# Gated delta rule: the queries' decay factors come as one row per head through memory, and VectorE multiplies them in at level 0 of the inverse

## What is computed

```python
gc = jnp.cumsum(to_chunks(g, l), axis=-1)          # log decays, summed within a chunk
...
sol = lax.linalg.triangular_solve(a_mat + jnp.eye(l), rhs, left_side=True, lower=True, unit_diagonal=True)
u, w = sol[..., :dv], sol[..., dv:]
qk = jnp.where(incl, jnp.einsum('bhnid,bhnjd->bhnij', qc, kc) * dmat, 0.0)
q_dec = qc * jnp.exp(gc)[..., None]                # the queries with their decay
...
def step(s, inp):
    v_new = u_i - jnp.einsum('bhck,bhkv->bhcv', w_i, s)
    o = jnp.einsum('bhck,bhkv->bhcv', q_i, s) + jnp.einsum('bhij,bhjv->bhiv', qk_i, v_new)
```

## Time and profile before

| | |
|---|---|
| time, median of 3 executions | 1592.13 us (1590.66 to 1593.95) |
| the profiled execution: its own time | 1594.32 us |
| its span, first to last instruction | 1592.6 us |
| busy in the span: PE, DVE, ACT, POOL | 1563.1, 1055.5, 884.4, 256.2 us |
| mean granted clock of PE | 0.994 of full speed |

### The profile page before, as it was taken

How to read it: one execution, slowest core, us unless ns; L and a number is a source line. 1 busy time by engine, 2 the same in 40 slices (tenths; PEclk the granted TensorE clock), 3 DMA queues, 4 the chain that set the end, 5 groups by cost and what they waited for, 6 DMA issues and landing times.

```text
span 1592.6 us, 37769 instructions
## 1 busy us (share of the span) xinstructions
PE 1563.1 (98%) x16212; PEld 1481.5 (93%) x16212; DVE 1055.5 (66%) x1732; ACT 884.4 (56%) x1696; POOL 256.2 (16%) x328
## 2 busy tenths in 40 slices
PE   9999999999999999999999999999999999999997
PEld 7998799999997999999788888999999997999997
DVE  7965686755757877547793747776469837767643
ACT  6856656633645666434652546665358547566433
POOL 7105450000110200003003421100010035400000
PEclk9999999999999999999999999999999999999999
DMA  8941456565753665653635003665569512565550
GB/s 244 292 140 29 134 164 179 183 206 175 255 160 133 200 176 185 195 185 94 189 96 144 20 7 98 176 185 186 186 182 261 174 55 82 165 181 184 188 167 28
DMA packets 245529, 250.10 MB, mean 157 GB/s; under 512 B 16270, under 2 KB 239284, under 8 KB 245300
## 3 DMA queue, kind: packets, MB, share of 16 engines
q1 hardware_dynamic: 237204, 224.78, 46.3%
q0 software_dynamic: 8016, 22.86, 4.9%
q10 hardware_dynamic: 144, 0.05, 0.0%
HBM read 229.75 MB, written 18.32 MB: 156 GB/s over the span
## 4 chain that ended last, share of the span: by engine, by line
PE 92%; ACT 4%; DVE 3%; issue 1%; DMA 0%; SPq 0%; DVEq 0%
PE ps L844 88%; PE ps L848 4%; ACT vk L2053 1%; ACT tri L2053 1%; ACT acts L2053 1%; ACT st L2053 0%; DVE acts L2760 0%; ACT hn L2053 0%; DVE tri L2752 0%; DVE acts L2752 0%; DMA acts<-in_x_sample_dram 0%; ACT L2056 0%; PE ps L1796 0%; DVE st L2760 0%; DVE hn L2760 0%
## 5 line engine op out<-in xcount | busy, mean ns | idle before, releaser
L2752 DVE TENSOR_TENSOR w_mlp<-ring,w_mlp 128x1024 fp32r<-128x1024 f32 x256 | 311.7, 1224 | 119.9 <-ACT w_mlp L2053 113.9
L2053 ACT ACTIVATE w_mlp<-ring 128x1024 fp32r<-128x1024 f32 x256 | 269.4, 1054 | 208.2 <-PE ps L844 208.2
L844 PE MATMUL ps<-hn_split,w_mlp 128*128 128x264 f32 x3072 | 373.3, 284 | 0.0
L844 PE MATMUL ps<-h_split,w_mlp 128*128 128x264 f32 x3072 | 372.6, 283 | 0.0
L844 PEld LDWEIGHTS ps<-hn_split,w_mlp 128*128 128x128 f32 x3072 | 372.0, 188 | 0.3
L844 PEld LDWEIGHTS ps<-h_split,w_mlp 128*128 128x128 f32 x3072 | 371.6, 188 | 0.0
L2053 ACT ACTIVATE tri<-ps 128x264 f32<-128x264 f32 (+4 forms) x222 | 101.4, 463 | 181.2 <-PE ps L844 156.2
L844 PE MATMUL ps<-gdn_hi,w_gdn 128*128 128x264 f32 x896 | 165.8, 285 | 0.0
L844 PEld LDWEIGHTS ps<-gdn_hi,w_gdn 128*128 128x128 f32 x896 | 139.3, 188 | 0.9 <-issue 0.8
L844 PE MATMUL ps<-mixer_lo,w_gdn 128*128 128x264 f32 x448 | 126.9, 283 | 0.0
L2752 DVE TENSOR_TENSOR tri<-tri 128x264 f32<-128x264 f32 (+4 forms) x145 | 59.7, 413 | 101.3 <-ACT h_split L2053 100.6
(11 more groups left out here) (454 smaller groups left out, 2654.2 us busy)
## 6 DMA issues: line engine op xcount, KB each, us to landing
ring<-in_ffn_w_dram SPq DMA_DIRECT2D x128, 1024.0 KB, 5.4
ring<-in_gdn_w_in_dram SPq DMA_DIRECT2D x32, 1024.0 KB, 8.3
ring<-in_ml_w_in_dram SPq DMA_DIRECT2D x12, 1024.0 KB, 5.5
ring<-in_rw_w_rkv_dram SPq DMA_DIRECT2D x12, 1024.0 KB, 5.0
st<-in_state_gdn_S_dram POOLq DMA_DIRECT2D x2, 4096.0 KB, 22.4
ring<-in_gdn_w_out_dram SPq DMA_DIRECT2D x8, 1024.0 KB, 5.0
out_gdn_S_s_dram<-st SPq DMA_DIRECT2D x16, 512.0 KB, 6.8
st<-in_state_mlstm_C_dram POOLq DMA_DIRECT2D x1, 4096.0 KB, 20.5
```

The source lines that it names most:

```text
L844: return nc.tensor.matmul(out, lhsT, rhs, start=start, stop=stop)
L2053: return nc.scalar.activation(out, in_, f, bias=bias, scale=scale)
L2752: return nc.vector.tensor_tensor(out, in0, in1, op)
```

## The change

The log factors of the queries are no longer spread over 128 partitions by PE. Instead, in `decay_exponents`, PE makes one product with 8 rows and 256 columns (one row per head), ACT takes its exponential into `row_exp`, writes these 8 KB to a new array in memory (`query_rows`), and POOL, behind `negC`, loads them back on all partitions at once: 1 MB into `QS`. The two `spread` calls of `decay_exponents` move behind the products on bank 7. POOL's eight multiplications go away; DVE does them, four in a new fill (0, 0), which begins with the wait for the load, and four in fill (0, 1) behind `sample_keys`. `statio`, the samples' operand of level 0, moves from tile A(6), where `QS` is, to A(7).

```diff
@@ PE, decay_exponents
-                    for half in range(2):
-                        spread(0, 4 + half, half)
+                    b = 4
+                    pe.wait_ge(*last_read[b])
+                    mm(ps[b][0:GH, 0:SEQ], selt[:, 4, :], RG[:, 0:SEQ]).then_inc(row_mm, count.up(row_mm))
+                    last_read[b] = row_ev, count.seen(row_ev)
                     b = 7
...
                     last.then_inc(cols_mm, count.up(cols_mm))
                     last_read[b] = cols_ok, count.expect(cols_ok)
+                    for half in range(2):
+                        spread(0, 4 + half, half)
@@ PE
-                def spread_queries():
-                    for q in range(4):
-                        b = 2 + q
-                        pe.wait_ge(*last_read[b])
-                        for n in range(2):
-                            last = mm(ps[b][:, n * SEQ:(n + 1) * SEQ], sel(4, 2 * q + n, P), RG[:, 0:SEQ])
-                        last.then_inc(qe_mm, count.up(qe_mm))
-                        last_read[b] = eq_ev, count.expect(eq_ev)
...
-                fills = {(0, 0): sample_products, (0, 1): spread_queries, (1, 0): sample_outputs,
+                fills = {(0, 0): sample_products, (1, 0): sample_outputs,
...
-                    if c == 1:
-                        pe.wait_ge(qs_ok, count.seen(qs_ok, 4))
@@ ACT, at tile 27, ahead of the wait for cols_mm
+                        ac.wait_ge(row_mm, count.seen(row_mm))
+                        act(row_exp, ps[4][0:GH, 0:SEQ], ACT.Exp).then_inc(row_ev, count.up(row_ev))
+                        ac.wait_ge(row_ev, count.own(row_ev))
+                        ac.dma_start(query_rows[j], row_exp).then_inc(row_out, count.up(row_out, 16))
@@ ACT, ahead of the inverse
-                for q in range(4):
-                    ac.wait_ge(qe_mm, count.seen(qe_mm))
-                    act(QS[:, 2 * q:2 * q + 2, :], ps[2 + q][:].rearrange("p (n t) -> p n t", n=2), ACT.Exp).then_inc(
-                        eq_ev, count.up(eq_ev))
@@ DVE
+                def decayed_queries(h0):
+                    for h in range(h0, h0 + 4):
+                        if not h:
+                            dv.wait_ge(spr_in, count.seen(spr_in, 16))
+                        part = QS[:, h, :].rearrange("p (a b t) -> p a b t", a=2, b=2)
+                        tt(part, part, rows_of(0, h), ALU.mult)
+
-                fills[0, 1], fills[1, 0], fills[1, 1] = sample_keys, sample_outputs, masked_values
+                fills[0, 0] = lambda: decayed_queries(0)
+                fills[0, 1], fills[1, 0], fills[1, 1] = lambda: (sample_keys(), decayed_queries(4)), sample_outputs, masked_values
@@ POOL
+                count.seen(row_ev)
+                po.wait_ge(row_out, 16 * (j + 1))
+                load(QS.rearrange("p h t -> p (h t)"), bc(query_rows[j].rearrange("h t -> (h t)"), P, 0), spr_in)
...
-                        po.wait_ge(eq_ev, count.seen(eq_ev))
-                        for h in (2 * l - 2, 2 * l - 1):
-                            part = QS[:, h, :].rearrange("p (a b t) -> p a b t", a=2, b=2)
-                            last = gp_.tensor_tensor(part, part, rows_of(0, h), ALU.mult)
-                        last.then_inc(qs_ok, count.up(qs_ok))
```

More of the change, by code:

```diff
@@ L276, in hybrid_trunk @@
         cum_ev = semaphore("cum_ev")
-        scan_ok = semaphore("scan_ok")
+        spr_in = semaphore("spr_in")
         dot_ev = semaphore("dot_ev")
@@ L417, in hybrid_trunk @@
         da_ok = semaphore("da_ok")
-        eq_ev = semaphore("eq_ev")
+        row_out = semaphore("row_out")
         kt_ev = semaphore("kt_ev")
@@ L444, in hybrid_trunk @@
         ot_mm = oq_mm
-        qe_mm = rt_mm
         smp_mm = h_mm
@@ L449, in hybrid_trunk @@
         ssq_ok = qs_ok
+        scan_ok = da_ok
+        row_mm = rt_mm
+        row_ev = rt_ok
         sums_mm = ct_mm
@@ L469, in hybrid_trunk @@
                     for i in range(2))
+        query_rows = [nc.dram_tensor(f"query_rows{n}", (GH, SEQ), F32, kind="Internal").ap() for n in range(2)]
+        row_exp = rows[0:GH, 4, 0:SEQ]
         QS = A(6).rearrange("p a b -> p (a b)")[:, 0:2 * D].rearrange("p (h t) -> p h t", h=GH)
-        statio = A(6).rearrange("p a b -> p (a b)")[:, 0:D].rearrange("p (h s n) -> p h s n", h=GH, s=NS)
+        statio = acts[:, 56:64, :].rearrange("p a b -> p (a b)")[:, 0:D].rearrange("p (h s n) -> p h s n", h=GH, s=NS)
         a7 = A(7).rearrange("p a b -> p (a b)")
@@ L1698, in rwkv @@
                     count.tiles += 2
+                count.expect(scan_ok, 4)
                 def sum_key_squares(q0):
```

## The result

The changed kernel takes 1604.31 us at the median of 5 executions (1603.08 to 1608.58). The kernel before takes 1592.13 (1590.66 to 1593.95). The ratio is 1.0084, with a 95% interval of 1.0073 to 1.0095: slower by 12.2 us at the medians, where +12.3 was forecast. The profiled execution took 1603.08 us, the lowest of the five (span 1601.4, granted clock 0.993). The profiled execution of before lies 2.2 us above its median, so the two spans differ by only 8.8 us (1601.4 against 1592.6).

A forecast was written before the change was run, and what follows sets the result against it. It took PE, busy for 98% of the span, to bound the kernel. The terms 2 x (4.1 + 0.46 + 1.6) = +12.3 us on a median of 1592.1 gave 1604.4, range 1596 to 1612.

The forecast's parts named there:

- The removed spreads: PE, level 1: eight products of 256 columns go, 3.65 us per layer.
- The row product: PE in `decay_exponents`: one added product of 256 columns costs 0.46 us per layer, bounds 0.40 to 0.50.
- ACT and the load: ACT's changes cost nothing; POOL's load takes 7 us, landing about 125, hidden with 13 us to spare.
- The first four: DVE's first four multiplications, 1.3 us or perhaps 2.7 with POOL's masks, are free in 4.84 us of idle time.
- The turns: DVE's second four multiplications and `krow_r` alternate with POOL's SBUF instructions; level 1's first subtraction moves from 143.75 to 148.85.
- no turns: Rival: the multiplications don't contend with POOL, and 3.2 us are gained, 1588.9; chance 0.07.
- fewer turns: Rival: DVE keeps its turn for its four multiplications, first subtraction at about 145.8; 1595 to 1599, chance 0.10.
- The second product set: PE, level 1: the second set starts at 151.05 instead of 146.94, +4.1 us per layer.
- The wait on PE: PE, level 1: after the key transposes it waits 7.7 us for bank 6.
- The clock: PE's wait brings a dip to half clock: +1.6 us per layer, bounds 0.5 and 3.2.
- row stage: `decay_exponents` on PE: forecast to grow by 0.46 us per layer, the new order of its products costing nothing.
- The clock stays low: Rival: the clock doesn't come back before the solve, up to 20 us a layer, say 1625; chance 0.10.

The follow-up runs named there:

- e1: The changed kernel with the load kept, but the eight multiplications back on GpSimd at levels 1 to 4; 1593.58 us, ratio 1.0009 to before.
- e2: The changed kernel with all eight multiplications on DVE in fill (0, 0); 1592.99 us, ratio 1.0006 to before.
- e5: The changed kernel with all eight multiplications in fill (0, 0) and GpSimd's state scaling one level later; 1589.21 us, ratio 0.9986 to before.
- e8: The changed kernel with the multiplications back on GpSimd at levels 1 to 4 and its state scaling one level later; 1589.64 us, ratio 0.9982 to before.
- e3: The changed kernel with GpSimd scaling only 4 of 128 columns of the states of levels 1 and 2; 1596.60 us, ratio 1.0023 to before.
- e4: The changed kernel with 12 idle products of 256 columns on PE, filling its wait for bank 6; 1599.22 us, ratio 1.0053 to before.
- e7: The changed kernel with GpSimd scaling each head's states one level later; 1600.87 us, ratio 1.0058 to before.

## Why the prediction was right

The median was right to 0.1 us, which is luck: the measured difference itself is uncertain by nearly 2 us either way, and the terms were off by more than 0.1. The mechanism was right. Point by point:

- **The removed spreads.** Right: they are gone, and 3.65 us of PE work with them. Level 1's first set starts 2.14 us behind level 0's last products; the prediction had about 1.1 (level 1 at 139.4). The 0.99 us of wait for DVE in PE's timeline was not foreseen: the first set writes a bank that DVE's second subtraction of level 0 has to release, and the spreads had hidden that. In the change it costs nothing, as it is used up by the longer wait; in e1, e2, e5 and e8 it is part of the path.
- **The row product.** Sized too small: +0.79 us per layer against 0.46, outside the bounds of 0.40 to 0.50. The product is 0.52; the other 0.27 came with the new order of the groups, which was costed at nothing.
- **ACT and the load.** Right: no wait, and 5.2 us to landing where 7 was taken.
- **The first four.** Right: in the cover, 2.69 us against "perhaps 2.7".
- **The turns.** The mechanism is right, and e3 shows it; e2 shows that it depends on the place. Its size was put too large: DVE's first level-1 subtraction moved by 4.32 us against 5.10. A mask holds a multiplication up for 1491 - 411 = 1.08 us, where 1.24 was used, and a scaling for 2112 - 411 = 1.70, where 1.85 was. The order of turns was as written, with one free multiplication at the end. The rival *no turns* is out; so is *fewer turns*, whose first subtraction would have come 6.3 us behind, not 8.61. The Trainium skill (SBUF — State Buffer, section Who interferes with whom) has the later instruction blocked until the first is done; the trace agrees, with 1.08 and 1.70 us.
- **The second product set.** +3.94 us against +4.1. Of these 3.94, 0.46 is already clock (the four transposes took 1.11 us; 0.66 in e4, whose second set comes 12.16 us behind, +3.48).
- **The wait on PE.** 5.85 us against 7.7. The difference is the smaller turns and the 0.99 us that PE now waits earlier.
- **The clock.** The dip came, and its term was near: from the value transposes to the second outer product PE took 157.27 - 149.17 = 8.10 us, and 6.66 in e4: 1.44 per layer, against 1.6. But the 1.6 was read from 3.4 us of low clock with PE busy throughout; what came was 6.8 us with PE busy for 5.13. Twice as long and less costly per us: that the two sizes nearly agree is luck.

So, by the profiles, the terms are 3.48 (wait), 0.79 (row stage) and 1.44 (clock), in sum 5.71 us per layer and 11.4 for both, where 4.1 + 0.46 + 1.6 = 6.16 and 12.3 were forecast. The row stage was too small by 0.33, the wait too large by 0.62. Over all executions, e4's medians give 4.7 us to the clock where 3.2 was forecast, and 7.5 to wait and row stage where 9.1 was; the intervals are too wide to set these apart from the forecast or from the profiles' 2.9 and 8.5. *The clock stays low* was not the rule, but one of its cases did occur, in e3.

Open: by their profiled timelines the inverse and the row stage gain about 1.7 us in e1 and 1.3 in e2, but the medians are 1.9 and 1.3 us above before's. Neither profile has a low stretch in the inverse, yet both have them elsewhere. In e2 the products of the solve, which follow the inverse and take 4.08 us at full clock, are slowed in both layers, where the kernel before has this in layer 3 only the earlier trace rows; in e1 the row stage of layer 3 takes 6.45 us against 4.82 in layer 0. PE's timeline of e2:

```profile
177.73 5.63 PE L848 MATMUL ps<-vk,tri 64*64 64x128 f32 x64
...
1345.13 5.66 PE L848 MATMUL ps<-vk,tri 64*64 64x128 f32 x64
```

Each such stretch costs about 1.6 us. A single profile doesn't say how often they come; over all executions the mean granted clock is a little lower (0.9957 and 0.9955; before 0.9969). Why it should be lower isn't shown, nor that it accounts for the whole gap of some 3 us. In e5 and e8 the clock is 0.9967 and 0.9963; the traces give gains of 3.3 and 3.6 us there, the medians 3.0 and 2.5.

## What to carry to other kernels

Work that one engine hands to another comes at two prices: its duration, and its turns with the engine that it leaves. Before moving an instruction with two SBUF operands to VectorE, count GpSimd's instructions in the stretch where it will stand: here four multiplications of 0.41 us in each of two layers cost 11 us more, clock included, where two masks and a scaling ran beside them than in idle time some 6 us earlier. When TensorE work is taken out of a dependent chain, look at what it covered, since the next wait (here for a bank, then for masks) decides how much of it is gained; and a wait that remains may cost more through the clock (here 1.44 us per layer beside 3.48).

## What the hardware showed beyond what was expected

- One hold per GpSimd instruction: multiplications that met none of them ran at their full speed (0.41 us) in the midst of slow ones. A hold was some 0.15 to 0.2 us shorter than GpSimd's instruction as the prediction counted it (1.08 against 1.24, 1.70 against 1.85), while GpSimd's own instruction grew by about 0.17 (in the changed kernel a mask from 1.27 to 1.44, a scaling from 1.90 to 2.07).
- `mvs`, one instruction of 1.22 us alone, took 2.91 in e5 beside the scaling: a long VectorE instruction paid one hold (1.69) like a short one.
- Beside the new product, the groups of the row stage took 0.27 us longer in their new order, though none of them was changed.
- The length of the low clock doesn't follow the length of TensorE's wait: 6.8 us behind waits of 5.85, 3.4 behind 4.4 (e7), and in one execution of e3 13.7 us behind a wait of 2.72 and 3.4 behind one of 2.73. Filling the wait of 5.85 with 12 products that nobody uses took 4.7 us off the median.
